# Where the split activations of a two-block decoder stack lie in SBUF: rows of 1024 and 1280 bytes instead of 1088

## What is computed

```python
def swiglu(x, w_gu, w_down):
    gate, up = jnp.split(x @ w_gu, 2, axis=-1)
    return (jax.nn.silu(gate) * up) @ w_down

def first_block(...):
    h = jnp.concatenate([meta, x], axis=1)
    for l in range(DEPTH):
        h = h + 0.5 * swiglu(rms_norm(h, ffn1_norm[l]), ffn1_w_gu[l], ffn1_w_down[l])
        u = rms_norm(h, mix_norm[l])
        ...
        h = h + merged @ w_out[l]
        h = h + 0.5 * swiglu(rms_norm(h, ffn2_norm[l]), ffn2_w_gu[l], ffn2_w_down[l])
    return rms_norm(h, final_norm)[:, N_META:]

def second_block(...):
    for l in range(DEPTH):
        x = macaron_ffn(x, ...)
        m = recurrent_block(...) if l < N_A_LAYERS else moba_attention(...) @ attn_w_o[j]
        x = x + rms_norm_2(m, mix_post_g[l])
        x = macaron_ffn(x, ...)
        if l == N_A_LAYERS - 1:
            k_blk, v_blk, k_mean = shared_kv(x, kv_norm_g, w_kv)
    return x
```

## Time and profile before

| What | Value |
|---|---|
| Median of 3 runs | 2403.17 us (2402.28 to 2404.51) |
| Profiled execution, its own time | 2404.25 us |
| Profiled execution, span | 2402.5 us |
| TensorE matmul busy | 2282.4 us, 95%, 18270 matmuls |
| VectorE busy | 1403.0 us, 58% |
| ScalarE busy | 1161.5 us, 48% |
| GpSimd busy | 554.1 us, 23% |
| DMA | 380.47 MB, mean 158 GB/s |

### The profile page before, as it was taken

How to read it: one execution, slowest core, us unless ns; L and a number is a source line. 1 busy time by engine, 2 the same in 40 slices (tenths; PEclk the granted TensorE clock), 3 DMA queues, 4 the chain that set the end, 5 groups by cost and what they waited for, 6 DMA issues and landing times.

```text
span 2402.5 us, 49086 instructions
## 1 busy us (share of the span) xinstructions
PE 2282.4 (95%) x18270; PEld 2243.1 (93%) x18270; DVE 1403.0 (58%) x1966; ACT 1161.5 (48%) x1752; POOL 554.1 (23%) x589
## 2 busy tenths in 40 slices
PE   7999999999999999999999999986999999978998
PEld 7999988999999999889999899976999999968998
DVE  6555856655555557766555565576653655465553
ACT  5444534454444436444554455466554455445553
POOL 4321000232213220001332232124430133112420
PEclk9999999999999999999999999997999999988999
DMA  6554423455545545233565465442664556533553
GB/s 214 177 187 155 140 88 115 133 175 175 186 147 185 183 157 158 92 98 119 166 193 192 141 192 190 146 161 80 194 205 145 200 181 197 168 104 106 186 192 113
DMA packets 99258, 380.47 MB, mean 158 GB/s; under 512 B 10911, under 2 KB 13087, under 8 KB 99016
## 3 DMA queue, kind: packets, MB, share of 16 engines
q1 hardware_dynamic: 99144, 378.91, 48.9%
HBM read 377.80 MB, written 3.16 MB: 159 GB/s over the span
## 4 chain that ended last, share of the span: by engine, by line
PE 85%; DVE 6%; ACT 3%; issue 2%; DVEq 2%; POOL 1%; POOLq 1%; DMA 0%; ACTq 0%; SPq 0%
PE bank L582 25%; PE bank L584 25%; PE bank L583 25%; ACT whi L976 2%; DVE wlo L1375 2%; PE bank L643 1%; PE bank L645 1%; PE bank L644 1%; PE bank L860 1%; POOLq L1936 1%; PE bank L600 1%; PE bank L770 1%; PE bank L849 0%; DVE cv L1711 0%; PE bank L839 0%
## 5 line engine op out<-in xcount | busy, mean ns | idle before, releaser
L1375 DVE TENSOR_TENSOR wlo<-raw,whi 128x1024 fp32r<-128x1024 f32 (+1 forms) x660 | 870.4, 1330 | 533.9 <-ACT whi L976 531.5
L582 PE MATMUL bank<-xhi,wlo 128*128 128x256 f32 (+1 forms) x3384 | 970.9, 287 | 5.5 <-DVE z L1727 3.9
L584 PE MATMUL bank<-xhi,whi 128*128 128x256 f32 (+1 forms) x3384 | 966.6, 286 | 0.0
L583 PE MATMUL bank<-xlo,whi 128*128 128x256 f32 (+1 forms) x3384 | 964.7, 285 | 0.0
L976 ACT ACTIVATE whi<-raw 128x1024 fp32r<-128x1024 f32 (+1 forms) x660 | 728.9, 1117 | 466.5 <-PE bank L584 432.7
L582 PEld LDWEIGHTS bank<-xhi,wlo 128*128 128x128 f32 x3384 | 642.2, 190 | 7.7 <-issue 5.7
L584 PEld LDWEIGHTS bank<-xhi,whi 128*128 128x128 f32 x3384 | 642.2, 190 | 0.0
L583 PEld LDWEIGHTS bank<-xlo,whi 128*128 128x128 f32 x3384 | 640.3, 189 | 0.0
L582 PE MATMUL bank<-hidhi,wlo 128*128 128x256 f32 (+1 forms) x1408 | 398.6, 283 | 0.0
L584 PE MATMUL bank<-hidhi,whi 128*128 128x256 f32 (+1 forms) x1408 | 398.3, 283 | 0.0
L583 PE MATMUL bank<-hidlo,whi 128*128 128x256 f32 (+1 forms) x1408 | 397.7, 282 | 0.0
(11 more groups left out here) (314 smaller groups left out, 2545.2 us busy)
## 6 DMA issues: line engine op xcount, KB each, us to landing
raw<-ffn_gu SPq DMA_DIRECT2D x352, 512.0 KB, 3.6
raw<-ffn_down SPq DMA_DIRECT2D x128, 704.0 KB, 4.1
raw<-mix SPq DMA_DIRECT2D x120, 512.0 KB, 3.5
raw<-rec SPq DMA_DIRECT2D x28, 512.0 KB, 3.9
raw<-kv SPq DMA_DIRECT2D x16, 512.0 KB, 3.8
raw<-att SPq DMA_DIRECT2D x16, 512.0 KB, 3.7
bias_rows<-rows SPq DMA_DIRECT2D x8, 256.0 KB, 4.3
bias<-bias_rows SPq DMA_DIRECT2D x1, 1536.0 KB, 8.6
```

Source lines behind the costliest of these rows:

```text
L582: pe.matmul(out, wlo[:, slot, w], xh(i), start=(i == 0), stop=False)
L583: pe.matmul(out, whi[:, slot, w], xl(i), start=False, stop=False)
L584: mm = pe.matmul(out, whi[:, slot, w], xh(i), start=False, stop=(i == last))
L1375: dve.tensor_tensor(wlo[:, k, 0:cols], raw[:, k, 0:cols], whi[:, k, 0:cols].bitcast(F32), ALU.subtract).then_inc(lo_made, 1)
```

## The change

`xhi`, `xlo`, `hidhi` and `hidlo` are no longer one tensor each. Each stage gets a view of its own on the same memory, and each view fixes where its rows begin. The views of one operand overlap, since no two stages need them at once; the arena grows by 1024 floats a partition.

- Stages of 256 columns use rows of exactly 256 columns, 1024 bytes, without room for the meta tokens. All their rows begin 64 bytes behind a multiple of 256. The feed-forward stage named F6 (the first of the second block's second layer) has such rows at 192.
- Stages of 272 columns use rows of 320 columns, 1280 bytes, of which 272 are used. Rows begin at 64 in the first feed-forward stage of a layer and in the mixers, at 192 in the second feed-forward stage of layer 0. Tiles of the second layer's mixer that need 256 columns read them from column 16 of such a row, at 128.
- The keys-and-values stage and the output product of the attention stage read `mid_tokens`, rows of 1024 bytes at 64, in place of `midhi` and `midlo`. The mixers' own `midhi`, `rechi`, `atthi` and `lathi` keep rows of 1088 bytes, and begin 64 bytes earlier modulo 256.
- Matmuls, their columns, their order and their waits are the same, and so are the weights' places. What lies behind the operands in the arena moves. VectorE gets four register instructions more in its program, since `h` and the operand now have rows of different length where a loop's counter picks the row.

```diff
-        arena = ctx.enter_context(nc.sbuf_tensor("arena", [P, 52176], F32))
+        arena = ctx.enter_context(nc.sbuf_tensor("arena", [P, 53200], F32))
...
+        LINE, SHIFT, BACK_SHIFT, ROW = 256, 64, 192, T + 48
+
+        def pair_at(name, count, first, cols):
+
+            return (at(name + "_hi", [P, count, cols], F32R, [first]),
+                    at(name + "_lo", [P, count, cols], F32R, [first + count * cols * 4]))
+
+        def line_after(place):
+            return (place + LINE - 1) // LINE * LINE
+
+        xbase = line_after(top[0])
+        x_tokens = pair_at("x_tokens", KD, xbase + SHIFT, SEQ)
+        X = {0: pair_at("x_first", KD, xbase + SHIFT, ROW), 1: pair_at("x_mixer", KD, xbase + SHIFT, ROW),
+             2: pair_at("x_second", KD, xbase + BACK_SHIFT, ROW), "last": x_tokens, "F4": x_tokens, "REC": x_tokens,
+             "F5": x_tokens, "F6": pair_at("x_back", KD, xbase + BACK_SHIFT, SEQ), "ATT": x_tokens, "F7": x_tokens}
+        top[0] = xbase + BACK_SHIFT + 2 * KD * ROW * 4
         h = at("h", [P, KD, T], F32)
-        xhi = at("xhi", [P, KD, T], F32R)
-        xlo = at("xlo", [P, KD, T], F32R)
...
-        hbase = top[0]
-        hidhi = at("hidhi", [P, KF, T], F32R)
-        hidlo = at("hidlo", [P, KF, T], F32R)
-        ebase = top[0]
+        hbase = line_after(top[0])
+        hid_tokens = pair_at("hid_tokens", KF, hbase + SHIFT, SEQ)
+        HID = {0: pair_at("hid_first", KF, hbase + SHIFT, ROW), 2: pair_at("hid_second", KF, hbase + BACK_SHIFT, ROW),
+               "last": hid_tokens, "F4": hid_tokens, "F5": hid_tokens,
+               "F6": pair_at("hid_back", KF, hbase + BACK_SHIFT, SEQ), "F7": hid_tokens}
+        hid_end, ebase = hbase + BACK_SHIFT + 2 * KF * ROW * 4, hbase + BACK_SHIFT + 2 * KF * SEQ * 4
...
-        H = [hbase]
+        H = [hbase + SHIFT]
...
+        mid_tokens = pair_at("mid_tokens", KD, hbase + SHIFT, SEQ)
...
+        def cut(t, k, c):
+
+            first = c if t.shape[-1] >= T else 0
+            return t[:, k, first:first + T - c]
...
-                                      lambda i: hidhi[:, i, c:T], lambda i: hidlo[:, i, c:T], waits,
+                                      lambda i: cut(HID[s][0], i, c), lambda i: cut(HID[s][1], i, c), waits,
...
-                        k8_tile(b + q, k, b * RING + j + k - 3, k, (xhi, xlo), c)
+                        k8_tile(b + q, k, b * RING + j + k - 3, k, X[s], c)
...
-                stage_tiles(q, j, x, n, (midhi, midlo), c, 8)
+                stage_tiles(q, j, x, n, mid_tokens, c, 8)
...
-                act.activation(to[:, at_k, c:T], h[:, at_k, c:T], ACT.Identity, scale=gain(x, k)).then_inc(x_hi_made, 1)
+                act.activation(cut(to, at_k, c), h[:, at_k, c:T], ACT.Identity, scale=gain(x, k)).then_inc(x_hi_made, 1)
```

More of the change, by code:

```diff
@@ L326, in program @@
         assert M[0] <= midbase + 2 * KD * T * 4
-        E0 = [ebase]
+        E0 = [hid_end]
         onehot = at("onehot", [P, 512], F32, E0)
@@ L676, in stage_tiles, with ffn @@
                         norm_back(n, c)
-            def ffn(q, j, x, n, f, c, layer, main_norm=True):
+            def ffn(q, j, x, n, f, c, layer, s, main_norm=True):
                 group = 3 if c else 2
-                first_tiles(q, group, (xhi, xlo), c, inputs_ready(x))
+                first_tiles(q, group, X[s], c, inputs_ready(x))
                 for t in range(group, 2 * RING):
-                    k8_tile(q + t // RING, t % RING, j + 4 if t == 7 else None, early_bank(t), (xhi, xlo), c)
+                    k8_tile(q + t // RING, t % RING, j + 4 if t == 7 else None, early_bank(t), X[s], c)
                     if t == (4 if c else 3) and main_norm:
@@ L716, in mixer @@
                     if (step, i) == ("tile", 0):
-                        first_tiles(q, 2, (xhi, xlo), 0, inputs_ready(x), input_norm(x, n, 0))
+                        first_tiles(q, 2, X[1], 0, inputs_ready(x), input_norm(x, n, 0))
                     elif step == "tile" and i > 1:
@@ L721, in mixer @@
                         t, parts = i, mixer_parts(i)
-                        hi, lo, at_k = sources.get(TILE[t][0], (xhi, xlo, 0))
+                        hi, lo, at_k = sources.get(TILE[t][0], (*X[1], 0))
                         waits = None
@@ L875, in recurrent @@
                 q, j, x, n, c = (REC[k] for k in "qjxnc")
-                stage_tiles(q, j, x, n, (xhi, xlo), c, 16)
+                stage_tiles(q, j, x, n, X["REC"], c, 16)
                 for t in range(16, 32):
@@ L909, in attention @@
                 q, j, x, n, c = (ATT[k] for k in "qjxnc")
-                stage_tiles(q, j, x, n, (xhi, xlo), c, 8)
+                stage_tiles(q, j, x, n, X["ATT"], c, 8)
                 pe.wait_ge(tile_read, j + 8)
@@ L933, in attention @@
                     t = 8 + m
-                    k8_tile(q + 2 + m // RING, m % RING, j + t - 1 if m >= 2 else None, 4 + m % 2, (midhi, midlo), c)
+                    k8_tile(q + 2 + m // RING, m % RING, j + t - 1 if m >= 2 else None, 4 + m % 2, mid_tokens, c)
                 post_norm(n + 1)
@@ L1118, in mixer @@
                         elif kind == "out":
-                            x_hi(x + 1, m, c)
+                            x_hi(x + 1, m, c, X[2 if l < DEPTH - 1 else "last"][0])
                         if t >= OUT:
@@ L1359, in _ @@
             ffn_down(**F5, post=12)
-            inputs_from_h(10, 10, N_META, midhi)
+            inputs_from_h(10, 10, N_META, mid_tokens[0])
             keys_values()
@@ L1502, in tile @@
                                                  ).then_inc(tile_read, 1)
-                        x_lo(x + 1, m, c)
+                        x_lo(x + 1, m, c, X[2 if l < DEPTH - 1 else "last"])
                     for ch in chunks_ended(t):
@@ L1664, in small, with update @@
                 return vec[:, bass.ds(l * 6 + VEC["small"] + k, 1)]
-            def update(n, done, weight, x=None, to=xlo, hi=xhi, next_q=None, c=N_META):
+            def update(n, done, weight, x=None, to=None, next_q=None, c=N_META):
                 def scaled(k, size=2):
@@ L1959, in ffn @@
                         at_i = bass.ds(i, 1)
[L1960 to L1961 removed]
+                        pool.tensor_tensor(cut(HID[s][1], at_i, c), z[:, 2 + p:3 + p, c:T],
+                                           cut(HID[s][0], at_i, c).bitcast(F32), ALU.subtract).then_inc(hid_lo_made, 1)
             def mixer(l):
```

102 lines of the change are left out of this document (49 added, 53 removed).

## The result

The changed kernel takes 2386.74 us, the median of 4 runs (2380.49 to 2389.72), where the kernel before takes 2403.16 (2402.28 to 2404.51, 4 runs): a ratio of 0.9928 with an interval of 0.9907 to 0.9948, 16.4 us less. The forecast was 2360 and 2328 to 2392. The sign was right and the time lies inside the range, but 43 us were forecast and 16 came. The profiled execution of the changed kernel took 2389.72 us, the slowest of its four, with a span of 2387.9 us.

A forecast was written before the change was run, and what follows sets the result against it. TensorE was taken as the bound, a stage lasting as long as its matmuls are apart. Terms summed to 45.5 us, 41.4 after halving some stages' share, giving 2362, forecast as 2360 us, range 2328 to 2392.

The forecast's parts named there:

- term 1: Gate and up matmuls of 256 columns at 64: 118.3 to 113.3 ns each, 21.8 us off.
- term 2: Hidden rows of 256 columns, without F6: 118.1 to 113.3 ns a matmul, 10.1 us off.
- rival of the slow speed: Every stage begins as `cvhi` did after its pause, at 117.8 ns: 13 us gained, 2392 us; chance 0.13.
- three signs of being wrong: 117 to 118 ns in F4, a speed jump within one stage, or TensorE idle ahead of `lo_made`.
- Terms 5 and 6: 272 columns: at 64, 123.3 ns, 9.3 and 1.7 us off; at 192, 126.7 ns, a loss of 1.6 us.
- the first rival: 272 columns find the fast speed too (120.4 ns), and F6 as well: 68 us off, 2335 us; chance 0.25.
- Term 4: F6, 256 columns at 192: 117.1 ns a matmul, 1.7 us off.
- Term 3: `mid_tokens`: 504 matmuls of keys and values and attention's output, 5.0 ns each, 2.5 us off.
- Term 7: The mixer's 480 matmuls at 128 and the stages' first tiles: no change.
- Term 8: Four more register instructions on VectorE and other places of `h`, `z` and constants: no change.
- The rival on the other side: Slower: a constant place holds the rotation's worst row in every matmul; 25 us more, 2428 us; chance 0.05.
- The place is not the cause: Rival: `outhi` is fast for something else in its stretch, so nothing changes, 2403 us; chance 0.07.

The follow-up runs named there:

- e3_all64: Changed kernel with layer 0's second stage and F6 moved from 192 to 64, and what lies behind the operands by 128 bytes: 2377.13 us.
- e7_both: `e3_all64` plus the added matmuls of `e1_turn`, in F6 behind the third tile, and also in REC, keys and values and attention: 2376.28 us.
- e11_turn0_kept: `e9_kept` with the three added matmuls at place 0, also in REC, keys and values and attention, none in F6: 2365.66 us.
- e1_turn: Changed kernel plus three matmuls at place 128 behind the norm's broadcast in "last", F4, F5, F7, and three at 0 in F6: 2366.42 us.
- e9_kept: `e1_turn` with layer 0's second stage and F6 at 64 instead of 192, everything behind the operands left in place: 2354.48 us.

## Why the prediction was right or wrong

- **The failed step is the choice of 113.3 ns in terms 1 and 2**, with its reason, "since `outhi` is the long unbroken stream, as these are". They are not unbroken: the norm's sum cuts each of the four behind the fifth tile and the broadcast behind the sixth, as the pause cut `cvhi`; behind the broadcast all four ran at 117.8 to their end. The prediction had both speeds of the earlier trace rows and the sentence that how the stream begins seems to choose, and took no account of what interrupts a feed-forward stage. Its rival of the slow speed, priced at 2392 with a chance of 0.13, is what happened in the long streams, and the time lies inside the range because the range took that rival in. Its remark against it ("runs on without pauses once it is under way") was wrong. At 117.8 term 1 is 2.2 us in place of 21.8, and term 2 0.6 in place of 10.1. Even the 0.6 is too much: the 528 hidden matmuls of a 256-column stage took 62.1 us before and after, 117.9 and 117.8 ns, and the 118.1 of the earlier trace rows was read from 36 of them. Two of the three signs of being wrong that it named came: 117 to 118 ns in F4, and jumps between two speeds within a stage.
- **Terms 5 and 6 held**: 123.3 and 126.7 ns to 0.1, and -3.6, +1.6 and -3.7 us in their three stages. The short rows were enough. That 272 columns find a distance near 120.4, the first rival, is not borne out at any of the seven places tried.
- **Term 4**: F6 ran at 117.8, not at the 117.1 read from seven matmuls: 984 x 0.5 + 528 x 0.3 = 0.7 us in place of 1.7. The runs at 64 showed 113.3 possible there too.
- **Term 3** is partly there: the stages of which it is part gained 1.0 and 1.4 us, and the keys' and values' tiles ran at 113.3 and at 117.8 by turns, with transposes between them.
- **Term 7** took the mixer's 480 matmuls at 128 at nothing. At 128 a stream is 120.0 ns. In the mixer the starts without a restart are 119.6 apart on the mean, 117.7 before, a loss of some 480 x 1.9 = 0.9 us, and layer 1's mixer gained only 0.4.
- **Term 8** held: TensorE waits no longer for VectorE than before. The groups of after have 4.4 us of idle time ahead of 1456 matmuls on `x_tokens`, where the earlier trace rows had 4.9 ahead of 1944:

```profile
L607 PE MATMUL bank<-x_tokens_hi,wlo 128*128 128x256 f32 x1456 | 410.9, 282 | 4.4 <-DVE z L1746 3.9 <-DVE wlo L1394 0.4
L607 PE MATMUL bank<-hid_tokens_hi,wlo 128*128 128x256 f32 x704 | 197.8, 281 | 0.0
```

- **The rival on the other side**, the worst of the rotation held in every matmul, was a real danger: 126.7 at 192 is that case for 272 columns, and `e4_weights`, with the weights 64 bytes further on, is at 2418.94 us. It missed here because 117.8 at 64 is still below 118.3.
- **"The place is not the cause"** falls with the table of places and with `e4_weights`.

By the formula of the Trainium skill's page "TensorE: Matmul & The Clock Gate", section "Back-to-back issue gap", 256 columns would be 256 / 2.4 + 2.5 = 109.2 ns apart, an estimate without a term for the address. The same section gives that formula for a matmul by itself and says that in a stream of weight loads and matmuls both set the spacing, which the prediction left out. The runs show 113.3 to 120.0 ns by place, none below 113.3. The same page's section "Step-by-step: what each phase is for" has weight loads on a read port of their own, taking nothing from the running matmul. `e4_weights` disagrees: a move of the weights alone made 117.8 into 118.7 at 64 and 123.3 into 126.7.

The four executions of the changed kernel spread over 9.2 us where the kernel before has 2.2. One stage that restarts fast is worth 6.4 us, so that would do it; only the slowest of the four has a trace, and it was not shown. The executions of `e3_all64`, `e7_both` and `e11_turn0_kept` spread over 9 to 12 us as well, those of `e1_turn` over 5.4 and of `e9_kept` over 2.4, and each kernel has one trace: what a stage did there may not be what it does in every execution. What decides a restart stays open.

## What to carry to other kernels

Where each matmul has weights of its own, read the distance between starts stage by stage, hundreds of matmuls apart; place operands relative to the weights, and try several places before settling on one. A speed read from an unbroken stream is not that of one which small matmuls of another kind, or a short wait, interrupt: compare the distance ahead of each interruption with the one behind it. Constant places are worth having only where the constant is below the mean of the rotation.

## What was not expected of the hardware

- One arrangement has two steady distances, 113.3 and 117.8 ns at 64, 117.3 and 120.0 at 32. 113.3, 117.8 and 117.3 were each kept over more than a thousand matmuls, 120.0 at 32 over some 90. Four small matmuls of a norm, three at another place, or a hitch of 0.1 us can move the stream from one to the other, and do not always.
- The distance depends on the operand's place less the weights' place: moving the weights by 64 bytes shifted the values that were compared by exactly 64 bytes.
- Between the fast and the slow stream the duration shown for a matmul moves from 277 to 282 ns, so the mean of a group is a hint of it too, as between the 1784 matmuls of `e9_kept` and the 1456 of the changed kernel.
